# The width of an expert's products chosen in eight short groups instead of once for the whole expert

## What is computed

```python
def moe_swiglu(h, w_router, b_router, w1, w3, w2):
    logits = h.astype(jnp.float32) @ w_router.astype(jnp.float32) + b_router.astype(jnp.float32)
    top_v, top_i = lax.top_k(logits, TOP_K)
    gates = jax.nn.softmax(top_v, axis=-1)
    comb = jnp.sum(jax.nn.one_hot(top_i, N_EXPERTS, dtype=jnp.float32) * gates[..., None], axis=-2)
    comb = comb.astype(h.dtype)
    y = jnp.zeros_like(h)
    for e in range(N_EXPERTS):
        y = y + comb[..., e:e + 1] * swiglu(h, w1[e], w3[e], w2[e])
    return y
```

## Time and profile before

| | us |
|---|---|
| runs (3) | 1732.95, 1733.9, 1734.55 |
| median | 1733.9 |
| the profiled execution | 1732.69 |
| its span | 1730.9 |
| first up product to last y transpose of the expert stage | 1081.7 to 1685.6 |

### The profile page before, as it was taken

How to read it: one execution, slowest core, us unless ns; L and a number is a source line. 1 busy time by engine, 2 the same in 40 slices (tenths; PEclk the granted TensorE clock), 3 DMA queues, 4 the chain that set the end, 5 groups by cost and what they waited for, 6 DMA issues and landing times.

```text
span 1730.9 us, 26002 instructions
## 1 busy us (share of the span) xinstructions
PE 1488.1 (86%) x11320; PEld 1425.0 (82%) x11320; DVE 600.9 (35%) x815; ACT 461.0 (27%) x646; POOL 398.0 (23%) x288
## 2 busy tenths in 40 slices
PE   5777794797999999998968784999999986999992
PEld 4555694697999999997957682999999986999992
DVE  6757598734102111014696622011110110010115
ACT  6767421433222122222313312111111110010114
POOL 1101571253344333443450512000000000000005
PEclk9999897899999999998988897999999997999995
DMA  9999231113423323233221027589789792658644
GB/s 319 326 308 348 67 98 32 41 59 118 126 74 100 108 74 98 58 101 98 74 73 49 6 71 271 193 272 334 242 286 318 271 309 76 216 164 300 228 146 169
DMA packets 249973, 286.70 MB, mean 166 GB/s; under 512 B 7469, under 2 KB 241599, under 8 KB 249814
## 3 DMA queue, kind: packets, MB, share of 16 engines
q1 hardware_dynamic: 244886, 272.17, 48.4%
q0 software_dynamic: 3760, 12.09, 1.9%
q10 hardware_dynamic: 1200, 0.56, 0.1%
HBM read 266.45 MB, written 19.07 MB: 165 GB/s over the span
## 4 chain that ended last, share of the span: by engine, by line
PE 71%; DVE 15%; DMA 5%; issue 4%; SPq 2%; ACT 2%; POOL 1%; POOLq 0%; DVEq 0%; ACTq 0%
PE PP L746 29%; PE PP L1014 21%; PE PP L1026 11%; DVE work L1499 7%; DMA mem<-in_w_ada 4%; PE PP L759 2%; PE PP L791 2%; DVE stat L1595 2%; PE PP L720 1%; PE PP L731 1%; PE PP L985 1%; PE PP L996 1%; DVE stat L1428 1%; DVE mem L1441 1%; DVE mem_r L1437 1%
## 5 line engine op out<-in xcount | busy, mean ns | idle before, releaser
L746 PE MATMUL PP<-hT_r,mem_r 128*128 128x260 f32 x2624 | 428.5, 284 | 4.6 <-DVE xT L1453 3.2
L1014 PE MATMUL PP<-big,mem 128*128 128x144 f32 (+2 forms) x2816 | 372.9, 295 | 22.8 <-issue 22.0
L1014 PEld LDWEIGHTS PP<-big,mem 128*128 128x128 f32 x2816 | 370.7, 191 | 23.5 <-issue 22.4
L604 POOL TENSOR_TENSOR mem_r<-mem,mem_r 128x1024 fp32r<-128x1024 f32 (+1 forms) x108 | 279.0, 2598 | 407.7 <-ACT mem_r L1141 407.0
L746 PEld LDWEIGHTS PP<-hT_r,mem_r 128*128 128x128 f32 x2624 | 362.5, 189 | 6.5 <-issue 2.5
L746 PE MATMUL PP<-mem_r 128*128 128x260 f32 x1312 | 263.8, 283 | 0.0
L746 PEld LDWEIGHTS PP<-mem_r 128*128 128x128 f32 x1312 | 201.7, 188 | 0.0
L1026 PE MATMUL PP<-big,mem 128*128 128x144 f32 (+2 forms) x1408 | 193.5, 294 | 0.0
L1026 PEld LDWEIGHTS PP<-big,mem 128*128 128x128 f32 x1408 | 186.6, 190 | 0.0
L1689 DVE TENSOR_TENSOR big<-PP,stat 128x256 f32<-128x256 f32 x88 | 37.4, 425 | 394.4 <-ACT stat L1324 394.4
L702 POOL DMA_INDIRECT mem<-y_by_expert,place x10 | 9.9, 986 | 624.5 <-SPq L534 621.8
(11 more groups left out here) (236 smaller groups left out, 1100.5 us busy)
## 6 DMA issues: line engine op xcount, KB each, us to landing
mem<-in_w_moe SPq DMA_DIRECT2D x48, 1536.0 KB, 8.8
mem<-in_w_ada SPq DMA_DIRECT2D x48, 1024.0 KB, 11.2
mem<-in_w_moe SPq DMA_DIRECT2D x32, 1408.0 KB, 9.4
mem<-in_w_dense SPq DMA_DIRECT2D x20, 1024.0 KB, 5.5
mem<-in_w_in SPq DMA_DIRECT2D x16, 1024.0 KB, 5.4
mem<-in_w_moe SPq DMA_DIRECT2D x16, 1024.0 KB, 6.8
mem<-in_w_dense SPq DMA_DIRECT2D x16, 704.0 KB, 4.7
mem<-in_w_out SPq DMA_DIRECT2D x8, 1024.0 KB, 5.1
```

The lines of the kernel that those rows point to most:

```text
L604: pool.tensor_tensor(r_(raw), raw, read_(hi), ALU.subtract).then_inc(w_lo, 1)
L746: mm = pe.matmul(PP[q][:, h, 0:HT], r_(w[:, k, :]), r_(x[:, k, HT * h:HT * h + HT]), start=(i == 0 and w is wh and x is hi), stop=(i == le ...
L1014: mm = pe.matmul(PP[w][:, f % 2, 0:n], raw[:, w, k, :], hn[:, k, 0:n], start=(k == 0), stop=(k == KD - 1))
```

## The change

Widths 128 and 136 are added, seven in all. The choice of width moves from the expert to its parts: `up` (c = 0 to 3) holds up to three blocks f, 48 products (32 in the last), `down` (c = 0 to 3) two blocks q, 22 products. `by_width` now builds, for each of the eight groups of an expert, a chain of compare-and-branches from the widest down to the narrowest, then the seven bodies one behind the other in rising width, each with a jump to the group's end. The waits for weights and for `hn` and all transposes move out of the bodies, between the groups. With that the transposes of y blocks 6 and 7 stand after the first up group of the next expert, and the others come in pairs after a down group. The branch hint is gone.

```diff
-WIDTHS = [144, 160, 176, 208, NW]
+WIDTHS = [128, 136, 144, 160, 176, 208, NW]
...
-            def expert(e, n, c):
-
-                for f in range(ET):
...
+            def up(e, c, n):
+
+                for f in range(3 * c, min(3 * c + 3, ET)):
...
-                    if f == 1 and e:
-                        y_tr(e - 1, KD - 1)
-                for q in range(KD):
-                    if q % 2 == 0:
-                        chunk_here(e, 8 + q // 2)
+
+            def down(e, c, n):
+
+                for q in (2 * c, 2 * c + 1):
...
-                    if q:
-                        y_tr(e, q - 1)
-                    if q in (3, 5) and e + 1 < NE:
-                        rows_tr(e + 1, (q - 3) // 2)
-                    if q == 3 and n < NW:
-                        over = pe.mark_branch_hint_location()
-                if n < NW:
-                    pe.br_lt(c, T + 1, on_true=f"expert_over{e}", on_false=f"expert_over{e}").branch_hint(over)
...
+            def by_width(e, part, c):
+
+                def among(widths):
+
+                    n = widths[-1]
+                    if len(widths) == 1:
+                        part(e, c, n)
+                        pe.br(f"{name}_over")
+                        return
+                    m = widths[-2]
+                    pe.br_lt(counts[e], m + 1, on_true=f"{name}_to_{m}", on_false=f"{name}_of_{n}")
+                    with nc.body(f"{name}_to_{m}", valid_engines=[pe.engine]):
+                        among(widths[:-1])
+                    with nc.body(f"{name}_of_{n}", valid_engines=[pe.engine]):
+                        part(e, c, n)
+                        pe.br(f"{name}_over")
...
             for e in range(NE):
-                by_width(e, counts[e], WIDTHS)
-                nc.switch_bb(f"expert_over{e}")
+                pe.wait_ge(R["hn_odd"], 2 * e + 2)
+                pe.wait_ge(R["hn_even"], 2 * e + 2)
+                for c in range(4):
+                    chunk_here(e, 2 * c)
+                    chunk_here(e, 2 * c + 1)
+                    by_width(e, up, c)
+                    if c == 0 and e:
+                        y_tr(e - 1, KD - 2)
+                        y_tr(e - 1, KD - 1)
+                for c in range(4):
+                    chunk_here(e, 8 + c)
+                    by_width(e, down, c)
+                    if c:
+                        y_tr(e, 2 * c - 2)
+                        y_tr(e, 2 * c - 1)
+                    if c in (1, 2) and e + 1 < NE:
+                        rows_tr(e + 1, c - 1)
```

More of the change, by code:

```diff
@@ L1025, in expert @@
                             pe.wait_ge(R["f_free"], ET * e + (ET - 1 if k == 0 else ET))
-                        mm = pe.matmul(PP[2][:, q % 2, 0:n], expert_slot(PER_E * e + 8 + q // 2, ET, 256)[:, k, P * (q % 2):P * (q % 2) + P],
+                        mm = pe.matmul(PP[2][:, q % 2, 0:n], expert_slot(PER_E * e + 8 + c, ET, 256)[:, k, P * (q % 2):P * (q % 2) + P],
                                        Gn[:, k, 0:n], start=(k == 0), stop=(k == ET - 1))
                     mm.then_inc(R["y_done"], 1)
-                    if q:
-                        y_tr(e, q - 1)
-                    if q in (3, 5) and e + 1 < NE:
-                        rows_tr(e + 1, (q - 3) // 2)
-                    if q == 3 and n < NW:
-                        over = pe.mark_branch_hint_location()
-                if n < NW:
-                    pe.br_lt(c, T + 1, on_true=f"expert_over{e}", on_false=f"expert_over{e}").branch_hint(over)
[L1037 to L1050, removed]
+            def by_width(e, part, c):
[12 more added lines that the diff above has]
+                        pe.br(f"{name}_over")
+                name = f"e{e}_{part.__name__}{c}"
+                among(WIDTHS)
+                nc.switch_bb(f"{name}_over")
             pe.wait_ge(R["count"], 2)
@@ L1056, in _ @@
             for e in range(NE):
-                by_width(e, counts[e], WIDTHS)
-                nc.switch_bb(f"expert_over{e}")
+                pe.wait_ge(R["hn_odd"], 2 * e + 2)
[15 more added lines that the diff above has]
+                        rows_tr(e + 1, c - 1)
+            y_tr(NE - 1, KD - 2)
             y_tr(NE - 1, KD - 1)
```

## The result

| | before | after |
|---|---|---|
| median, us (4 runs each) | 1734.08 | 2060.07 |
| lowest to highest | 1732.95 to 1734.55 | 2054.49 to 2062.4 |
| profiled execution, us (its span) | 1732.69 (1730.9) | 2062.4 (2060.6) |
| expert stage: first up product to last y transpose | 603.9 | 932.3 |
| of it TensorE idle | 22.2 | 269.8 |

The changed kernel takes 1.1875 times as long, 95% interval 1.1856 to 1.1893. The forecast was 2000 us with a range of 1850 to 2090; the run lies inside it, 60 us above the forecast.

What follows compares the result with a forecast made beforehand. TensorE's products bound the expert stage, with holes from missing instructions, not weights. From 1732.7 us, -22.0 - 28.2 + 271 + 16 + 30 = +267 gave 1,999.7, so 2,000 us; range 1,850 to 2,090.

Steps and rivals of the forecast that it cites:

- Part 1, the old holes: Expert stage: TensorE's instruction waits ahead of experts 5 and 6 go, since their branches no longer exist; -22.0 us.
- Part 2, narrower products: Experts 0, 2 and 7 go to width 128, 1 and 4 to 136, at 1.667 ns a column; -28.2 us.
- Part 3, the choices: The 64 unhinted group choices: nearly every group has one far jump; +271 us, plus 16 for jumps meeting a load.
- The cover: Work queued on TensorE while its sequencer runs ahead, about 16 instruction pairs, hides 1.8 us of a jump at width 128.
- the two-packet picture: A far jump brings the target's packet and the next; 250 to 500 instructions can be reached without a fetch.
- the bound of 1,886: Forecast's own lower bound in us: 3.35 us a far jump, nothing for the clock, the rest as it is.
- The clock (+30): TensorE's clock halves for a while after some gaps; 0.5 us a gap, +30 us, bounds 0 and 102.
- Part 4, moved steps at no cost: Transposes of y blocks 6 and 7, moved into the next expert's up part, and the reordered y store cost nothing.
- Rival 1: Instruction reach is a block longer, so down-group jumps of 528 and less mostly avoid the fetch; 1,862 us, chance 18%.
- Rival 2: Everything within about 1,160 instructions ahead is held, so no group's jump shows; 1,682 us, chance 6%.
- Rival 3: 50 far jumps meet a load under way and nearly every gap halves the clock; 2,179 us, chance 7%.
- What would show it: Signs in the changed profile: some 60 branches of 4 to 8 us, "issue" idle of some 250 us, over 200 packets.

Runs made afterwards that it cites:

- experiment 9: Kernel before with seven widths, one body per expert, the next expert's width chosen early and its branch hinted: 1687.9 us, ratio 0.9735 to before.
- Experiment 8: Changed kernel with eight more products of 256 columns, results unread, ahead of each group's end jump: 2216.55 us, ratio 1.2772 to before.
- Experiments 5 and 6: Changed kernel and kernel before, in that order, each with width 208 alone and so without a choice: 1899.86 and 1900.44 us.
- experiment 7: Changed kernel with widths 144 and 208 alone, so every jump goes over one body of a group: 1730.88 us, ratio 0.9983 to before.
- experiment 11: Changed kernel with one block a group, 19 groups an expert, and widths 128, 144 and 208 alone: 1752.1 us, ratio 1.0108 to before.

## Why the prediction came out as it did

**What bounds the kernel** was read rightly: the stage lasts as long as TensorE's products and TensorE waits for instructions, not weights. With the jumps gone (experiment 9) its idle time is 2.1 us.

**Part 1, the old holes (-22.0).** The 22.2 us of idle time of before belong to branches that are gone. Right.

**Part 2, narrower products (-28.2).** Measured -24.6 at full clock. The step that was a little off is the price at 128. In experiment 9 expert 7's 144 up products behind the first 32 began at 1586.04 and the down part at 1618.19:

```profile
1586.04:1618.19 32.15, 32.15 (x290) 32.15 (x289) 5.02 (x11) 3.42 (x9) 0.00 (x0) 1.00 0.76 248
```

32.15 / 144 = 223.3 ns, where the line through 144 and 208 gave 218.3. Over 792 products that is 4.0 us that the last eight columns don't bring. The transposes of 110 ns each bear out a pass of 112 ns (half of 223.3) as well as one of 109, so they could not show that there is no floor, as I had them do.

**Part 3, the choices (+271, and +16 for jumps that meet a load).** Measured +269.8 of idle time, so 17 us under the two terms. By width, forecast (without the 16) against measured: 128 (experts 0, 2, 7) 98 and 82.4; 136 (1, 4) 67 and 83.5; 144 (3) 41 and 46.5; 160 (6) 44 and 43.8; 208 (5) 21 and 13.6. The sum is right by luck: two errors cancel.

The price of a far jump was too high: I took 4.95 us from before's four rows, and 47 of the 84 took 3.2 to 4.1, nearer the 3.35 that I kept as the lower bound; the mean of the 84 is 4.19. The cover was too small as well: TensorE went on for 2.15 us after the start of the jump in 20 of 24 cases at width 128, where I took 1.8.

The number was too low, 84 where my terms hold about 70: at 136 I charged 0.2 us for the jump ahead of the body, which goes over one body only, and it was far in 9 of 16 groups; at 144 I charged ten far jumps in all and there were 14; at 160 eleven and a half, and there were 13.

I had the two-packet picture of the Trainium skill (Runtime: NRT & Kernel Launch, Instruction fetch mechanics: a taken branch whose target is outside a window of two blocks waits for a load) and took it that both blocks are always there; the short jumps that were far speak against that. The jumps of 446 instructions and more agree with the page's window and not with its other figure, room for 2,048 instructions: of those of the changed kernel one took 1.8 us and all others 3.3 or more.

Of the dearer jumps that I charged 16 us for (12 cases of 7.6 us) there were more than twice as many, 27 of 4.8 us and up, but none as long as 7.6. 19 of the 27 began within 1.1 us of the landing of another far jump, which is the place that I had in mind.

Two slips in my arithmetic changed little: 60 jumps at 1.6 us less are 96 and not 84 us, so the bound of 1,886 should be 1,874; and by its own rule the cover at 160 and 208 is 2.2 and 2.8 us, not 2.3 and 2.9.

**The clock (+30): this is the term that was furthest off.** Measured +86.0. My upper bound of 102 holds it, my price does not. I priced 60 gaps of 2.6 to 4.2 us at 0.5 us each, from two single gaps of before, one of which had cost nothing. I overlooked before's third, the hole of 19.54 us: the clock was 0.50 for the 3.6 us behind it. The changed kernel has 79 gaps over 1 us, at 1.1 us each; 23 of them last 4 to 9 us, 20 of these in the experts with jumps ahead of and behind the bodies. These four experts (1, 3, 4, 6) lost 13 to 19 us each to half clock, 61 in sum; the other four lost 5 to 8. A single gap's cost does not carry over to a stage in which gaps return: the group at 1432.24 ran at 0.86 behind one at 0.82 and ahead of one at 0.82. By shape, over the whole stage, the up products of width 144 and of 208 in after (busy us, mean ns of one record, idle ahead):

```profile
L1008 PE MATMUL PP<-big,mem 128*128 128x144 f32 x352 | 53.4, 322 | 28.7 <-issue 28.7
```

```profile
L1008 PE MATMUL PP<-big,mem 128*128 128x208 f32 x352 | 66.6, 353 | 9.7 <-issue 7.9 <-DVE big L1697 1.8
```

The 352 records of width 144 took 43.36 us in before and 53.4 here, 23% more, with 28.7 us of gaps ahead of them. Those of 208 would take 61.9 (176 x 351.7 ns, rows 4) and took 66.6, 8% more, with 9.7 us of gaps. Experiment 8 shows the same from the other side, at its experts 7 and 4.

**A term that the sum lacked (+19.3).** Products were held at full clock too, the first behind a gap above all, as shown with the result. I had nothing for them.

**Part 4, moved steps at no cost.** Experiments 5 and 6 agree to 0.6 us. Right.

The sum again: 267 - 17 (idle, Part 3) + 56 (clock) + 19 (products held at full clock) + 4 (Part 2) + 1 (outside) = 330.

**The rivals.** Rival 1 (a block more of reach) fell: all 24 end jumps at width 128 were far, the down ones of 535 instructions among them with 3.3 to 5.2 us. Rival 2 (everything within 1,160 instructions is held) fell with the same rows; what is true of it is that jumps of 90 to 194 instructions are free in code that runs on (experiment 7). Rival 3 (full traffic) was half true: its clock term of 90 us was the better one (86), but its waits were not there, 27 jumps of 4.8 us or more and not 50 of 7.6.

**What would show it.** Far branches: 84 instead of 60, most shorter than the 4 to 8 us announced. "Issue" idle of some 250 us: 220 ahead of the products on the page, the rest ahead of transposes. Instruction packets over 200: 233. Products at 128 of 218 ns: 223. Clock below 1.00: 0.86.

## What to carry to other kernels

A choice made on the chip costs by whether TensorE's program jumps out of the instructions that are already there, and by how often, not by its compares: make it rarely, put the compares in a row ahead of the bodies, ask for the next choice early, and hint the one branch that will be taken some 10 us ahead. Where it must be made often, keep the jump under some 200 instructions and let no far jump stand shortly ahead of it; that made it free with two widths (experiment 7), and not quite with three bodies a group (experiment 11). Jumps of 446 and up cost 3.3 us or more in the changed kernel in all cases but one. Count a gap on TensorE twice where gaps return: once as idle time, and once for the slower products behind it (270 and 107 us here).

## What the runs showed of the hardware

- In the changed kernel a jump over 446 instructions or more, without a hint, took 3.3 us or more in all cases but one (1.8), and its price did not grow with the distance: the nine of 1,159 took 3.3 to 4.1 us, seven of the eight of 446 at a group's end 3.3 to 3.8 and one 6.35. Of the 27 that took 4.8 to 7.1 us, 19 began within 1.1 us of another far landing; of the other 57 far ones, one did.
- A jump of 90 instructions took 0.19 to 0.32 us or 3.9 to 5.6 in one and the same kernel; the long ones all began within 1.1 us of a far landing.
- A hint for a branch that is taken needs a lead: under 4.2 us it didn't hide the load in any of 16 cases, with 8.2 us and more it did in 8 of 9.
- Behind a gap of 2.7 us (1093.67 to 1096.37) 48 products of width 128 took 10.99 us, 0.3 more than in a steady run (48 x 223.3 ns), with the granted clock at 1.00. Behind gaps of 5.5 to 8.8 us 48 products of width 144 took 14.0 to 14.7 us instead of 11.8.
- A product of 128 columns took 223.3 ns, 5 ns more than the line through 144 and 208 columns gives.
